# A streaming encoder layer with an expert mixer: state stores after the value weights' load, that load in halves, an earlier forget gate Exp, the mixer's loops written out, and the sample's queries in halves at later slots

## The chip, the cores and the metric

The kernel runs on one core of one Trainium2 chip. The metric is the device time of one execution in microseconds (us), lower is better. Three executions of the kernel before took 3363.31 to 3365.3 us, median 3364.35 us.

## The reference, cut to what matters

One layer over a prompt of 1024 tokens and a sample of 32 tokens, width 1024. A combined input projection feeds an RG-LRU group and an mLSTM group (4 heads of 128), an output projection closes the mixer of time, and a PEER block with 16384 experts closes the layer.

```python
def mlstm_chunk(carry, inp):              # per head, in chunks
    b = jnp.cumsum(lf, axis=-1)           # lf = log_sigmoid(forget gate)
    logD = jnp.where(causal, b[..., :, None] - b[..., None, :] + ig[..., None, :], -jnp.inf)
    m_t = jnp.maximum(inter, jnp.max(logD, axis=-1))
    ...
    C_new = w_c[..., None, None] * C + jnp.einsum('bhs,bhsd,bhse->bhde', w_k, k, v)

def peer(h, wq, k1, k2, u, v):            # 8 heads, 16 experts a head and token
    q = (xb @ wq).reshape(PEER_BLOCK, PEER_HEADS, D_QUERY)
    q = q * lax.rsqrt(jnp.mean(q * q, axis=-1, keepdims=True) + EPS)
    s1 = jnp.einsum('phd,kd->phk', q1, k1); s2 = jnp.einsum('phd,kd->phk', q2, k2)
    v1, i1 = lax.top_k(s1, 16); v2, i2 = lax.top_k(s2, 16)
    sv, si = lax.top_k((v1[..., :, None] + v2[..., None, :]).reshape(..., 256), 16)
    expert = e1 * N_KEYS + e2
    g = jax.nn.softmax(sv, axis=-1)
    act = jax.nn.gelu(jnp.einsum('phkd,pd->phk', jnp.take(u, expert, axis=0), xb))
    return jnp.einsum('phk,phkd->pd', g * act, jnp.take(v, expert, axis=0))

def trunk_layer(...):
    h = rmsnorm(x, norm1_w) * (1.0 + sc1) + sh1
    z = h @ w_in + b_in
    ya, h_last, conv_new = rglru(...); yb, C, n, m = mlstm(...)
    x = x + g1 * (jnp.concatenate([ya, yb], axis=-1) @ w_out)
    h2 = rmsnorm(x, norm2_w) * (1.0 + sc2) + sh2
    return x + g2 * peer(h2, ...), h_last, conv_new, C, n, m
```

## The kernel before, in words

The order of the work is written out by hand, one program for each engine, and semaphores tie the programs together. The 1056 tokens stand in 9 tiles (`NT`): 8 of 128 prompt tokens and one of 32 sample tokens.

**First part.** PE (TensorE) multiplies 16 blocks of 128 columns of the input projection (`lb`, line 686): the LRU's xa and ga, then q and k. The key blocks k0 to k3 come last; behind k1 stand the input and forget gates (line 697). ACT (ScalarE) evicts each block (lines 1031 and 1033). Then come the value and output-gate columns, `value_gate`, in 18 units: most are 8 products of 128x512 (line 743), the unit for the sample tile is 32 products of 128x256 (line 737) and needs both weight halves, `wo` and `wv`. `wo` is loaded early; `wv` takes the SBUF slots 4 to 7 of the block weights and is loaded by SP (line 424) once block k3 is done (`z_mm` at `VO`, 51). DVE (VectorE) adds the biases and evicts (lines 1483 and 1492); a PSUM bank must be evicted before PE's unit four later may start in it.

The forget gate's log-sigmoid needs |f| (DVE, line 1510), Exp of it (ACT, line 1087), then a log1p of 13 operations on 4 rows of 1056 (DVE, lines 1300 to 1308). In DVE's program this stands ahead of the first eviction, `evict_vo(0)`. In ACT's program the Exp stands behind all block evictions.

POOL (GpSimd) issues the small transfers. Ten of them (`store`, line 508) write the LRU states to HBM, column by column of SBUF, so that each element is a piece of 4 bytes of its own: two of 128x4 and eight of 128x3. They stand ahead of `top_dram` (line 516) and of its broadcast back, `top_b` (line 536). Later `store_state(1, 1)` writes the sample's mLSTM state, and DVE's `carry(1)` (line 1593) waits for 14 stores together (`SAMPLE_STORES`) before it overwrites that state. Then follow mLSTM, output projection and second norm over the 9 tiles, with PE's program the longest.

**Second part, the mixer.** A slot is one expert of each token of a tile: POOL gathers 128 rows of 8 KB (line 588, an indirect DMA of 1 MB) into one of 8 ring buffers, DVE takes the dot product with the token (`dot`, line 1809), ACT makes the weight and puts it on a diagonal (`weight`, lines 1232 to 1240), and PE multiplies the diagonal with the second half of the rows into PSUM (`mix`, line 915), which frees the buffer (`v_free`). There are 128 slots a prompt tile (8 heads h of 16 slots j) and 32 for the sample tile, 1056 in all. In between, two heads ahead, PE makes the next queries (`query`, line 884) and scores (lines 904, 906) and DVE sorts them (`route` steps). ACT's `query` (line 1199) copies the query out of PSUM; it stands behind `weight` of slot 0. At `h == S_AT` (5) of the head two ahead, that is while head 3 is mixed, `query` also multiplies the sample's 32 tokens with this tile's head of weights (line 891, 16 products of 128x32 in one piece), in eight tiles once.

`each_tile` sets the tiles in the programs of POOL, ACT and DVE: tile 0, then a hardware loop of three rounds of two tiles (1 to 6), then tiles 7 and 8. SP has a loop of its own around `finish`. PE's program is written out.

```python
            tile(0, 0, P, P)
            with eng.Fori(0, (NT - 3) // 2) as i:
                tile(i * 2 + 1, 1, P, P)
                tile(i * 2 + 2, 0, P, P)
            tile(NT - 2, 1, P, DEC)
            tile(NT - 1, 0, DEC, None)
```

## Time and profile before

| | |
|---|---|
| median of three executions | 3364.35 us |
| the profiled execution | 3363.62 us |
| its span, first to last instruction | 3361.8 us |
| PE busy, weight loads | 86%, 42% |
| DVE, ACT, POOL busy | 66%, 64%, 36% |
| moved by DMA | 1191.56 MB, of it 1118.53 MB by POOL's queue |
| instruction fetches in the span | 264 packets, 2.80 MB |

The span is cut into two: the first 610 us or so, in which PE is busy nearly all the time and DMA little, and the mixer behind it, in which the DMA engines are busy in nearly every slice and every other engine has gaps. A busy share over the whole span mixes both.

### The profile page before, as it was taken

What the parts mean: (1) busy time and instruction counts of PE and PEld (TensorE: products, weight loads), DVE (VectorE), ACT (ScalarE), POOL (GpSimd) and SP (SyncE); (2) the same over time, 40 slices, a digit from 0 to 9 for tenths busy, and PEclk for the clock granted to TensorE, in tenths of its full rate; (3) what the DMA queues carried; (4) which work ended last, traced back from release to release, by engine and by line L of the source; (5) the groups of instructions that cost most, each with busy time, mean ns of one, the idle gap of its engine ahead of it and who ended that gap; (6) DMA issues with size and microseconds to landing.
All of it is one profiled execution on the core that took longest, in us unless ns stands there. A gap on an engine that the chain in (4) does not pass through costs nothing. (4 is left out here: it accounts for less than half of the span.)

```text
span 3361.8 us, 42448 instructions
## 1 busy us (share of the span) xinstructions
PE 2888.0 (86%) x9454; PEld 1410.6 (42%) x9454; DVE 2231.8 (66%) x5472; ACT 2150.2 (64%) x7214; POOL 1206.9 (36%) x1134
## 2 busy tenths in 40 slices
PE   7998999788888888888888888888888888888886
PEld 5664455434434443343344334343443343434331
DVE  5685355667676667666666676666666766676665
ACT  3332133477776777677667776777777777777775
POOL 0001000244444444344435444444444444434443
PEclk9999999899999999999999999999999999999999
DMA  7233032799999999999999999999999999999998
GB/s 280 85 114 62 30 119 79 322 420 412 419 417 414 396 419 409 407 411 419 389 413 415 419 417 394 419 419 387 402 420 419 415 392 419 420 415 400 420 419 330
DMA packets 169996, 1191.56 MB, mean 354 GB/s; under 512 B 20027, under 2 KB 21467, under 8 KB 30211
## 3 DMA queue, kind: packets, MB, share of 16 engines
q0 software_dynamic: 155792, 1118.53, 81.0%
q1 hardware_dynamic: 13940, 70.23, 5.9%
q8 instruction: 78, 1.28, 0.2%
q14 instruction: 186, 1.52, 0.1%
HBM read 1179.42 MB, written 9.25 MB: 354 GB/s over the span
## 5 line engine op out<-in xcount | busy, mean ns | idle before, releaser
L915 PE MATMUL ps<-r_w,r_yT 128*128 128x512 f32 (+1 forms) x3168 | 1525.7, 616 | 329.7 <-ACT r_yT L1240 326.5
L1809 DVE SCALAR_TENSOR_TENSOR r_yT<-r_w,r_qk 128x1024 bf16<-128x1024 f32 x792 | 968.9, 1225 | 683.8 <-DMA r_w<-in_peer_uv,gidx 682.7
L588 POOL DMA_INDIRECT r_w<-in_peer_uv,gidx x792 | 872.9, 1102 | 1018.1 <-PE ps L915 895.4
L915 PEld LDWEIGHTS ps<-r_w,r_yT 128*128 128x128 f32 (+1 forms) x3168 | 551.8, 189 | 1216.0 <-issue 1214.9
L915 PE MATMUL ps<-r_yT 128*128 128x512 f32 (+1 forms) x1056 | 526.6, 633 | 87.3 <-ACT r_yT L1240 76.1
L588 POOL DMA_INDIRECT r_yT<-in_peer_uv,gidx x264 | 291.6, 1104 | 559.3 <-PE ps L915 490.9
L1232 ACT ACTIVATE mixc<-mixc 128x1 f32<-128x1 f32 x1056 | 207.2, 196 | 441.3 <-DVE r_yT L1809 437.6
L1240 ACT ACTIVATE r_yT<-ident,mixc 128x128 f32<-128x128 f32 x1024 | 411.2, 402 | 97.7 <-ACT mixc L1236 5.1
L1236 ACT ACTIVATE mixc<-mixc 128x1 f32<-128x1 f32 x1056 | 409.1, 387 | 35.0
L1235 ACT ACTIVATE mixc<-mixc 128x1 f32<-128x1 f32 x1056 | 408.3, 387 | 33.8
L1809 DVE SCALAR_TENSOR_TENSOR r_yT<-r_yT,r_qk 128x1024 bf16<-128x1024 f32 x264 | 322.9, 1225 | 119.2 <-DMA r_yT<-in_peer_uv,gidx 102.5
L915 PEld LDWEIGHTS ps<-r_yT 128*128 128x128 f32 (+1 forms) x1056 | 198.7, 202 | 377.2 <-issue 376.8
L1234 ACT ACTIVATE mixc<-gate,mixc 128x1 f32<-128x1 f32 x1056 | 295.8, 280 | 0.0
L686 PE MATMUL ps<-r_hT,r_w 128*128 128x384 f32 (+1 forms) x768 | 232.8, 465 | 2.1 <-DVE r_hT L1403 1.8
L1233 ACT ACTIVATE mixc<-mixc 128x1 f32<-128x1 f32 x1056 | 198.3, 188 | 0.0
L686 PEld LDWEIGHTS ps<-r_hT,r_w 128*128 128x128 f32 x768 | 146.6, 192 | 87.0 <-issue 6.2
L1199 ACT ACTIVATE r_yT<-ps 128x256 f32<-128x256 f32 x64 | 24.5, 383 | 174.6 <-PE ps L884 129.9
L884 PEld LDWEIGHTS ps<-r_wq,r_vo 128*128 128x128 f32 x1024 | 120.9, 194 | 14.9 <-issue 14.8
L884 PEld LDWEIGHTS ps<-r_wq,r_hT 128*128 128x128 f32 x1024 | 119.4, 192 | 15.3 <-issue 15.3
L884 PE MATMUL ps<-r_wq,r_vo 128*128 128x128 f32 x1024 | 121.2, 277 | 0.0
L884 PE MATMUL ps<-r_wq,r_hT 128*128 128x128 f32 x1024 | 119.5, 275 | 0.0
L743 PE MATMUL ps<-r_w,r_hT 128*128 128x512 f32 x256 | 111.2, 593 | 0.0
(287 smaller groups left out, 2321.3 us busy)
## 6 DMA issues: line engine op xcount, KB each, us to landing
r_w<-in_ada_w SPq DMA_DIRECT2D x18, 1024.0 KB, 5.2
r_w<-in_peer_uv,gidx POOLq DMA_INDIRECT x792, 13.8
r_w<-in_w_lin SPq DMA_DIRECT2D x16, 512.0 KB, 7.4
r_yT<-in_peer_uv,gidx POOLq DMA_INDIRECT x264, 11.8
r_vo<-in_x_prompt SPq DMA_DIRECT2D x8, 512.0 KB, 7.3
r_qk<-in_ada_w SPq DMA_DIRECT2D x2, 2048.0 KB, 16.8
r_w<-in_w_vo SPq DMA_DIRECT2D x2, 2048.0 KB, 13.1
r_w<-in_w_out SPq DMA_DIRECT2D x2, 2048.0 KB, 8.4
```

The source lines that it names most:

```text
L588: pool.indirect_dma_start(ring[place(h, j)], None, table, bass.IndirectOffsetOnAxis(gidx_t[:, h, j:j + 1], 0))\
L686: m = nc.tensor.matmul(ps[:, bank, 0:n], wblk[:, nblk % 8, k, :], hT[:, k, c0:c0 + n], start=k == 0, stop=k == KD - 1)
L743: m = nc.tensor.matmul(ps[0:r, bank, :], hT[:, k, t * P:t * P + r], w[:, k, :], start=k == 0, stop=k == KD - 1)
L884: mm = nc.tensor.matmul(ps[:, 4, c * P:(c + 1) * P], wqs[h][:, k, c * P:(c + 1) * P], h2T[:, p, k, :], start=k == 0, stop=k == KD - 1)
L915: mm = nc.tensor.matmul(ps[0:r, 2 * p + c, :], diag[:, j % 4, 0:r], row[:, D + c * 512:D + (c + 1) * 512], start=h == 0 and j == 0, stop=h ...
L1232: nc.scalar.activation(sq[:, i:i + 1], d, ACT.Square, scale=(TANH_K * GELU_C) ** 0.5)
L1233: nc.scalar.activation(kd[:, i:i + 1], d, ACT.Copy, scale=TANH_K)
L1234: wch.link(nc.scalar.activation(gd[:, i:i + 1], gate_t[:, h, j:j + 1], ACT.Copy, scale=d))
L1235: wch.link(nc.scalar.activation(th[:, i:i + 1], sq[:, i:i + 1], ACT.Tanh, scale=d, bias=kd[:, i:i + 1]))
L1236: wch.link(nc.scalar.activation(wc[:, i:i + 1], th[:, i:i + 1], ACT.Identity, scale=gd[:, i:i + 1], bias=gd[:, i:i + 1]))
L1240: nc.scalar.activation(diag[:, j % 4, 0:r], (ident if r == P else sel32)[:, 0:r], ACT.Copy, scale=wc[:, i:i + 1]).then_inc(dg_ready, 1)
L1809: V.scalar_tensor_tensor(udump[j % 2], ring[i][:, 0:D], 1.0, h2[:, t, :], ALU.mult, ALU.mult, accum_out=dots[:, i:i + 1]).then_inc(dot_don ...
```

## The change

- **Stores.** The ten LRU state stores stand in POOL's program behind the broadcast of `top_b`, and wait for both halves of `wv` first.
- **Value weights.** `wv` is loaded in two halves: slots 4 and 5 once block k1 is done (`z_mm` 42), slots 6 and 7 once k3 is done (51). PE's first use waits for both (32).
- **Forget gate.** ACT's Exp stands behind the eviction of k2, ahead of that of k3.
- **Mixer.** `each_tile` has no loop: the programs of POOL, ACT and DVE hold all nine tiles, and SP's `finish` loop is written out as well.
- **Sample queries.** `S_AT` is 4, now the head being mixed; the 16 products stand in two pieces of 8, behind `mix` of slots 6 and 10. ACT copies them behind `weight` of slot 13, and PE waits for that copy before the query of the next head.

```diff
-S_AT = 5
+S_AT = 4
...
+        def each_tile(tile):
+            for t in range(NT):
+                tile(t, t % 2, rows(t), rows(t + 1) if t + 1 < NT else None)
...
-            for n, dst in ((1, wo), (0, wv)):
-                if n:
-                    sp.wait_ge(half_done[0], 8)
-                    sp.wait_ge(half_done[1], 8)
-                else:
-                    sp.wait_ge(z_mm, VO)
-                sp.dma_start(dst, A["w_vo"][n].rearrange("p (k n) -> p k n", k=KD)).then_inc(vo_ld[n], 16)
+            sp.wait_ge(half_done[0], 8)
+            sp.wait_ge(half_done[1], 8)
+            sp.dma_start(wo, A["w_vo"][1].rearrange("p (k n) -> p k n", k=KD)).then_inc(vo_ld[1], 16)
+            w_v = A["w_vo"][0].rearrange("p (k n) -> p k n", k=KD)
+            for q, blocks in enumerate((42, VO)):
+                sp.wait_ge(z_mm, blocks)
+                sp.dma_start(wv[:, 4 * q:4 * q + 4], w_v[:, 4 * q:4 * q + 4]).then_inc(vo_ld[0], 16)
...
             finish(0, P, x1_t[0], y_t[0])
-            sp.wait_ge(y_st, 16)
-            with sp.Fori(1, NT - 2) as t:
+            for t in range(NT - 2):
                 finish(t, P, x1_t[t], y_t[t])
...
             pool.dma_start(top_b, top_dram[:, :].partition_broadcast(P)).then_inc(top_ld, 16)
+            pool.wait_ge(vo_ld[0], 32)
             pool.wait_ge(lru_y, 2 * FT)
             for s in range(2):
                 store(outs[2 + 5 * s][0, 0].rearrange("(f p) -> p f", p=P), hl[:, s, :])
                 for f in range(FT):
                     store(outs[3 + 5 * s][0, 0, :, f * P:(f + 1) * P].rearrange("r p -> p r"), cvn[:, s, f, :])
...
-                if h == S_AT:
-                    if t == 0:
-                        pe.wait_ge(s_ev, 1)
-                    for c in range(2):
-                        for k in range(KD):
-                            mm = nc.tensor.matmul(ps[:, 4, 2 * P + c * DEC:2 * P + (c + 1) * DEC],
-                                                  wqs[t][:, k, c * P:(c + 1) * P], h2Ts[:, k, :],
...
+            def query_for_sample(t, c):
+                if t == 0:
+                    pe.wait_ge(s_ev, 1)
+                for k in range(KD):
+                    mm = nc.tensor.matmul(ps[:, 4, 2 * P + c * DEC:2 * P + (c + 1) * DEC],
+                                          wqs[t][:, k, c * P:(c + 1) * P], h2Ts[:, k, :],
+                                          start=k == 0, stop=k == KD - 1)
+                if c == 1:
+                    mm.then_inc(s_tr, 1)
...
+                    if h == S_AT + 1 and t < NT - 1:
+                        pe.wait_ge(s_ev, t + 2)
...
+                        if h == S_AT and t < NT - 1 and j in (6, 10):
+                            query_for_sample(t, j // 10)
...
+                if b == "k2":
+                    act.wait_ge(f_abs, 1)
+                    nc.scalar.activation(nmr, wst, ACT.Exp, scale=-1.0).then_inc(f_exp, 1)
...
-            act.wait_ge(f_abs, 1)
-            nc.scalar.activation(nmr, wst, ACT.Exp, scale=-1.0).then_inc(f_exp, 1)
...
+                        if r == P and h == S_AT and j == 13:
+                            queried_for_sample(t)
```

The issues of POOL, behind the last block of the projection; `out<-prm` are state stores. Before:

```order
L503 DMA r_wq<-in_state_mlstm_n 128x4x1
L508 DMA out<-prm 128x4x1
L508 DMA out<-prm 128x3x1 x4
L508 DMA out<-prm 128x4x1
L508 DMA out<-prm 128x3x1 x4
L516 DMA top_dram<-r_yT 4x1056
L508 DMA out<-prm 4x1 x2
L536 DMA r_yT<-top_dram 128x4224
L542 AFFINE_SELECT r_hT<-r_hT 32x4x32
```

Now:

```order
L497 DMA r_wq<-in_state_mlstm_n 128x4x1
L505 DMA top_dram<-r_yT 4x1056
L502 DMA out<-prm 4x1 x2
L525 DMA r_yT<-top_dram 128x4224
L502 DMA out<-prm 128x4x1
L502 DMA out<-prm 128x3x1 x4
L502 DMA out<-prm 128x4x1
L502 DMA out<-prm 128x3x1 x4
L538 AFFINE_SELECT r_hT<-r_hT 32x4x32
```

The ten stores of columns moved from ahead of `top_dram` to behind the load of `top_b`; the causal cut of the decays stands right behind them.

ACT at the end of the projection; `r_qk<-ps,prm` evicts a key block, the row on `r_w` of 4x1056 is the forget gate's Exp. Before:

```order
L1031 ACTIVATE r_qk<-ps,prm 128x3x128 x2
L1031 ACTIVATE r_qk<-ps,prm 128x2x128
L1033 ACTIVATE r_qk<-ps,prm 128x32
L1087 ACT_TABLE_LOAD
L1087 ACTIVATE r_w<-r_w 4x1056
L1084 ACTIVATE r_vo<-r_vo 32x512
```

Now:

```order
L1083 ACT_TABLE_LOAD
L1083 ACTIVATE r_w<-r_w 4x1056
L1033 ACTIVATE r_qk<-ps,prm 128x3x128 x2
L1033 ACTIVATE r_qk<-ps,prm 128x2x128
L1035 ACTIVATE r_qk<-ps,prm 128x32
L1089 ACTIVATE r_vo<-r_vo 32x512
```

The Exp with its table load passed the three evictions of k3.

PE in tile 1 of the mixer, at the sample's query; rows on `r_w` or `r_yT` of 128x512 are `mix`, two of them a slot, 128x128 x16 is a query, 128x32 the sample's. Before:

```order
L915 MATMUL ps<-r_yT 128x512 x4
L915 MATMUL ps<-r_w,r_yT 128x512 x12
L884 MATMUL ps<-r_wq,r_hT 128x128 x16
L891 MATMUL ps<-r_hT,r_vo 128x32 x16
L915 MATMUL ps<-r_yT 128x512 x4
```

Now:

```order
L914 MATMUL ps<-r_w,r_yT 128x512 x8
L889 MATMUL ps<-r_hT,r_vo 128x32 x8
L914 MATMUL ps<-r_w,r_yT 128x512 x2
L914 MATMUL ps<-r_yT 128x512 x4
L914 MATMUL ps<-r_w,r_yT 128x512 x2
L889 MATMUL ps<-r_hT,r_vo 128x32 x8
L914 MATMUL ps<-r_w,r_yT 128x512 x10
L880 MATMUL ps<-r_wq,r_hT 128x128 x16
```

The sample's products left the place behind an ordinary query, and stand in two pieces four slots apart in the next head.

## Rows read from the trace of the kernel before

**Rows 1.** Windows in the mixer: length, busy by engine, granted clock, DMA share, GB/s

```profile
660.00:760.00 100.00, 86.11 (x264) 40.31 (x263) 68.64 (x180) 70.56 (x247) 43.23 (x40) 0.98 1.01 419
...
760.00:800.00 40.00, 36.03 (x128) 18.46 (x127) 29.70 (x79) 29.33 (x105) 16.56 (x16) 1.00 1.00 405
1080.00:1120.00 40.00, 36.35 (x134) 19.45 (x134) 27.06 (x69) 28.86 (x104) 17.93 (x16) 0.96 0.91 373
1410.00:1450.00 40.00, 36.01 (x134) 18.61 (x132) 26.57 (x68) 28.47 (x102) 17.07 (x16) 1.00 0.95 377
1740.00:1780.00 40.00, 35.24 (x133) 18.86 (x134) 27.59 (x72) 28.33 (x103) 16.42 (x15) 1.00 1.00 399
2070.00:2110.00 40.00, 37.24 (x135) 19.68 (x134) 26.56 (x71) 28.81 (x105) 17.06 (x16) 0.96 0.93 384
2405.00:2445.00 40.00, 38.29 (x134) 20.30 (x132) 25.24 (x68) 27.80 (x101) 17.38 (x15) 0.91 0.96 384
2735.00:2775.00 40.00, 37.42 (x135) 19.50 (x133) 26.02 (x69) 28.45 (x102) 19.17 (x16) 0.96 0.93 378
3060.00:3100.00 40.00, 36.08 (x136) 19.43 (x135) 27.57 (x72) 28.76 (x105) 17.06 (x15) 1.00 0.96 381
```

**Rows 2.** The same view at three of the tiles' boundaries

```profile
1600.00:1660.00 60.00, 47.68 (x131) 21.18 (x130) 43.97 (x113) 42.46 (x145) 24.87 (x22) 0.94 0.94 376
2260.00:2320.00 60.00, 50.83 (x133) 22.96 (x134) 43.65 (x111) 42.92 (x147) 25.05 (x22) 0.91 0.94 374
1300.00:1360.00 60.00, 49.13 (x140) 21.57 (x139) 42.21 (x112) 45.38 (x148) 24.45 (x23) 0.97 1.00 404
```

**Rows 3.** Timeline, tile 1 at the sample's query: start, length, engine, line [idle before <-releaser]

```profile
1089.60 3.66 PE L891 MATMUL ps<-r_hT,r_vo 128*128 128x32 f32 x32
...
1093.29 0.38 ACT L1199 ACTIVATE r_yT<-ps 128x256 f32<-128x256 f32 x1 [5.50 <-PE ps L891]
...
1097.27 1.57 POOL L588 DMA_INDIRECT r_yT<-in_peer_uv,gidx  x1 [9.27 <-PE ps L915]
```

**Rows 4.** The same view, POOL at an ordinary head of tile 2

```profile
1463.30 0.94 POOL L588 DMA_INDIRECT r_yT<-in_peer_uv,gidx  x1 [4.29 <-PE ps L915]
```

**Rows 5.** The same view, DVE where the loop goes back to tile 3

```profile
1625.27 1.23 DVE L1809 SCALAR_TENSOR_TENSOR r_yT<-r_yT,r_qk 128x1024 bf16<-128x1024 f32 x1 [6.56 <-issue]
```

**Rows 6.** Landing times of line 424's two loads, SP's `wo` and `wv`

```profile
DMA to landing us min/median/max: 7.3/13.1/18.9
```

**Rows 7.** Timeline of PE, a value unit, the sample unit, and a shape like it

```profile
305.13 7.03 PE L743 MATMUL ps<-r_w,r_hT 128*128 128x512 f32 x16
...
324.40 5.86 PE L737 MATMUL ps<-r_w,r_hT 128*32 128x256 f32 x64 [12.24 <-DMA r_w<-in_w_vo]
...
458.68 1.91 PE L822 MATMUL ps<-r_w,r_hT 128*32 128x256 f32 x32
```

**Rows 8.** Window over that sample unit, columns as in Rows 1

```profile
324.40:330.20 5.80, 5.80 (x65) 3.06 (x65) 5.63 (x6) 0.00 (x0) 0.00 (x0) 0.61 0.01 3
```

**Rows 9.** Timeline of ACT and DVE around the forget gate

```profile
291.50 0.28 ACT L1033 ACTIVATE r_qk<-ps,prm 128x32 f32<-128x32 f32 x1
...
306.00 1.28 ACT L1087 ACT_TABLE_LOAD   x1
...
308.41 0.70 DVE L1300 TENSOR_SCALAR r_w<-r_w 4x1056 f32<-4x1056 f32 x1 [21.67 <-ACT r_w L1087]
...
331.47 0.69 DVE L1492 TENSOR_TENSOR r_vo<-ps,r_wr 128x512 f32<-128x512 f32 x1
```

**Rows 10.** Line 508, landing times of its last two LRU stores

```profile
DMA to landing us min/median/max: 24.1/25.2/26.4
```

**Rows 11.** Timeline, line 508's LRU stores, `top_b`, and DVE's `carry(1)`

```profile
285.34 7.44 POOL L508 DMA_DIRECT2D out<-prm  x10
...
388.38 0.56 POOL L536 DMA_DIRECT2D r_yT<-top_dram  x1 [28.40 <-PE ps L713]
...
431.20 1.50 DVE L1593 SCALAR_TENSOR_TENSOR r_wq<-r_wq,prm,ps 128x129 f32<-128x129 f32 x4
```

More of the change, by code:

```diff
@@ L536, in _ @@
             pool.dma_start(top_b, top_dram[:, :].partition_broadcast(P)).then_inc(top_ld, 16)
+            pool.wait_ge(vo_ld[0], 32)
+            pool.wait_ge(lru_y, 2 * FT)
+            for s in range(2):
+                store(outs[2 + 5 * s][0, 0].rearrange("(f p) -> p f", p=P), hl[:, s, :])
+                for f in range(FT):
+                    store(outs[3 + 5 * s][0, 0, :, f * P:(f + 1) * P].rearrange("r p -> p r"), cvn[:, s, f, :])
             def cut_future(i):
@@ L590, in tile @@
                             .then_inc(e_ld[place(h, j)], 16)
-            each_tile(pool, tile)
+            each_tile(tile)
             pool.wait_ge(out_st, n_out[0])
@@ L949, in tile @@
                             scores(ta, ha)
+                        if h == S_AT and t < NT - 1 and j in (6, 10):
+                            query_for_sample(t, j // 10)
                         if rn == P and h == 5 and j in (4, 10):
                             turn(t + 1, j // 10, rn)
-            for t in range(NT):
-                tile(t, t % 2, rows(t), rows(t + 1) if t + 1 < NT else None)
+            each_tile(tile)
         @block.scalar
@@ L1199, in query, with queried_for_sample @@
                 nc.scalar.activation(qts[:, :, :], q, ACT.Copy)
-                if h == S_AT:
-                    for c in range(2):
-                        nc.scalar.activation(qs[c].rearrange("p (h t) -> p h t", h=HEADS)[:, t, :],
+                nc.scalar.activation(qsq[:, :, :], q, ACT.Square).then_inc(q_sb, 1)
+            def queried_for_sample(t):
+                act.wait_ge(s_tr, t + 2)
+                for c in range(2):
+                    m = nc.scalar.activation(qs[c].rearrange("p (h t) -> p h t", h=HEADS)[:, t, :],
                                              ps[:, 4, 256 + c * DEC:256 + (c + 1) * DEC], ACT.Copy)
-                nc.scalar.activation(qsq[:, :, :], q, ACT.Square).then_inc(q_sb, 1)
+                m.then_inc(s_ev, 1)
             def query_sample(h):
@@ L1274, in tile @@
                             norm(number(ta, ha))
-                        if h == 0 and j == 8 and (not isinstance(t, int) or t >= 1):
-                            final_root(t + (-1))
+                        if h == 0 and j == 8 and t >= 1:
+                            final_root(t - 1)
                         if rn == P and h == 5 and j in (7, 13):
                             turned(t + 1, j // 13, 1 - p, rn)
-            each_tile(act, tile)
+                        if r == P and h == S_AT and j == 13:
+                            queried_for_sample(t)
+            each_tile(tile)
             final_root(NT - 1)
@@ L1874, in tile @@
                     n = number(t, h)
-                    fin = h == 0 and (not isinstance(t, int) or t >= 1)
+                    fin = h == 0 and t >= 1
                     dot(t, h, 0)
@@ L1913, in tile @@
                     if fin:
-                        final_scale(t + (-1), P)
+                        final_scale(t - 1, P)
                     if ra:
@@ L1927, in tile @@
                         experts(ha)
-            each_tile(dve, tile)
+            each_tile(tile)
             final_sum(NT - 1, 0, DEC)
```

34 lines of the change are left out of this document (10 added, 24 removed).

## The prediction

> **What bounds the kernel now.** I read the windows first, then the timeline at the places where a window falls off. In the mixer an undisturbed window moves 419 GB/s with the DMA engines full (share 1.01) [rows 1]. A slot is a gather of 128 rows of 8 KB, 1.05 MB, so it takes 1.05 MB / 419 GB/s = 2.50 us, and 1056 of them take 2640 us: four fifths of the profiled execution. In the same window PE is busy 86 of 100 us, ACT 71 and DVE 69, so none of them sets the pace. The time of the mixer changes only where the DMA engines run dry. That happens at two kinds of place.
>
> Once in each of eight tiles a window of 40 us falls to 373 to 405 GB/s [rows 1]. The timeline shows why: the sample's products keep PE for 3.66 us behind an ordinary query, ACT waits 5.50 us for them before it may go on to the next weights, no ring buffer comes free, and POOL sits 9.27 us without issuing a gather [rows 3]. At an ordinary head, with its own query of 16 products but without the sample's, POOL sits 4.29 us [rows 4], and the windows show no loss. So the gathers already queued cover a gap of about 4 us and not one of 9.
>
> At the starts of tiles 3 and 5, where the loop goes back, windows of 60 us fall to 376 and 374; at the start of tile 2, inside the loop's body, a like window has 404 [rows 2]. DVE stands 6.56 us on "issue", that is on nothing but its own program, ahead of the first dot product behind the jump [rows 5].
>
> Ahead of the mixer PE is the long program, and it has one large hole: 12.24 us for `wv` [rows 7]. The two loads of line 424 are of equal size and took 7.3 and 18.9 us [rows 6]; the slow one waits for k3, behind which PE goes on at 305.13 [rows 7], while the ten LRU stores of 4-byte pieces, issued from 285.34 on [rows 11], are still landing: the last two take 24.1 and 26.4 us [rows 10], to about 318 us.
>
> **The change part by part.** The sum is made against the profiled execution, 3363.62 us, which is 0.7 us under the median of 3364.35; I take them as one.
>
> *Stores and `wv`: 12.2 us.* Without the stores `wv`'s first half lands long before it is wanted. The second half is issued at about 305.2 us as before; PE wants it at 324.40 - 12.24 = 312.16 us. Half the bytes can hardly take longer than the 7.3 us of the whole undisturbed load, and 305.2 + 7.3 = 312.5, so at most 0.3 us of the wait is left and I take none. The Trainium skill, page DMA: Bandwidth & Descriptors, section Anatomy of one DMA, gives (for DMAs of POOL) each DMA a fixed cost of about 2.0 us beside its bytes. That speaks against loading in halves; by its fit the second half takes about 4.4 us, an estimate from the page, and is hidden all the same.
>
> *Clock: 2.0 us.* Behind the hole the sample unit ran at a mean granted clock of 0.61 [rows 8], partly at the lower level of 1.2 GHz, after PE had stood idle; its 64 instructions took 5.86 us, while 32 of the like shape later took 1.91 us [rows 7], so 3.8 us for 64 [rows 7]. With no hole there is nothing to fall from.
>
> *Forget gate: nothing by itself, but it guards these 14 us.* DVE's log1p starts at 308.41, when the Exp is done, and DVE's first eviction is at 331.47 [rows 9]. If the hole went alone, PE would do the sample unit to 316.0, one value unit of 7.03 us [rows 7] to 323.0, and then stand for the bank of unit 0, evicted at about 332.2: 9.2 us of 14.2 would come back as that wait. Now the Exp follows k2's eviction: 291.50 + 0.28, then load and Exp for 308.41 - 306.00 = 2.4 us [rows 9], so 294.2, before k3's first group is there. DVE starts 14.2 us earlier and evicts at 317.3. PE needs that bank at 323.0 and has 5 us in hand. ACT's wait for |f| costs nothing, since DVE was waiting for the Exp from 308.41 - 21.67 = 286.7 on.
>
> *Stores in their new place: +1.0 us.* Everything behind the hole moves 14.2 us up: `top_b` is issued at 374.2, the stores follow for 7.44 us of POOL [rows 11], covered by `top_b`'s landing, for which the decays and the causal cut wait anyway. The old batch took from 285.34 to 318.4 to land, 33 us, `wv` beside it in part; behind `top_b` the new one ends at 408 to 416. `store_state(1, 1)` queues behind it, and `carry(1)`, due at 431.20 - 14.2 = 417.0 [rows 11], waits for all 14. That wait is 0 to about 5 us on DVE; behind DVE stand evictions that PE wants some microseconds later. Bounds 0 and 5, taken 1, being nearer to no wait.
>
> *Sample queries: 23.5 us.* The eight windows lack 14, 46, 42, 20, 35, 35, 41 and 38 GB/s of 419, together 271; times 40 us / 419 is 25.9 us of empty DMA [rows 1]. A piece is half of 3.66 us [rows 3], 1.83 us; PE's spare time is 14 us in 100 us, or 0.35 us a slot, so four slots take back 1.4 us between the pieces. The gap that reaches POOL is then near the ordinary 4.29 us and not 9.27, and ACT's copies, behind slot 13, wait for nothing. PE's new wait ahead of the next query is for a copy issued two slots before. Bounds: 25.9 if nothing is left, 13 if the two pieces leave half. I take 0.3 us left a tile, 23.5.
>
> *Loops: 10.4 us.* The two windows lack 43 and 45 GB/s over 60 us: 6.2 + 6.4 = 12.6 us. What an ordinary boundary costs is between 0 and the 15 GB/s of tile 2's, 2.1 us [rows 2]; I leave 1.1 us at each. Bounds 8.3 and 12.6. The instructions executed are the same, and the page's totals show 264 fetch packets for all 42448 of them, loop rounds included, so there is no more to fetch. SP's loop waits for nothing that another engine feels.
>
> Sum: 12.2 + 2.0 - 1.0 + 23.5 + 10.4 = 47.1 us. 3363.6 - 47.1 = 3316.5; forecast **3316.5 us**.
>
> **The rivals.**
> 1. *The pieces stall as well* (10%). Head 4 also has ACT's table loads for the norm at slot 6, and PE's backlog of two pieces may add to them. For it: a gap of 9.27 us runs the queue dry and 4.29 does not, and the limit between is not shown. Against: each piece is shorter than an ordinary query. Half the gain gone: 3316.5 + 12 = 3328.5.
> 2. *The jump is not what costs* (7%). The Trainium skill, page Advanced Engine Details and Errata, section Control Flow Timing, puts a compare-and-branch at about 108 ns; by that the edge would be cheap. As a mechanism of this kernel: DVE's stall is a fetch of instructions that straight code would meet as well. Against: DVE's stall stands right at the jump [rows 5], and the other edge's window reads like this one's, while tile 2's start, with no jump, reads 404 [rows 2]. Then 10.4 us stay: 3326.9. The row contradicts the page's figure if that is taken as the whole cost of an edge.
> 3. *The early gain is handed back* (10%). The store batch delays `carry(1)` by its full 5 us, or PE meets a bank not evicted. Half of 13.2: 3323.1.
> 4. *Slower than before* (2%). Straight programs for DVE, ACT and POOL may stall at each refill of their instructions while the DMA queues are full. The place is tiles 1 to 6; the price of a stall is DVE's 6.56 us [rows 5]. It decides from eight stalls on, 52 us against the other 47: at two a tile, 12 x 6.56 = 79, less the 10.4 that the loop no longer saves counted in, 3316.5 + 79 = 3395. Against it: tile 0 and tiles 7 and 8 are straight code already, and the window in tile 0 has 419 GB/s [rows 1].
> 5. *More than forecast* (8%): no residue at all, 3316.5 - 2.4 - 2.2 - 1.0 = 3310.9.
>
> **How the numbers follow.** The forecast itself has 63%; its terms alone span 3311 to 3323. For 8 in 10 I take in rivals 1, 2 and 3 and the lower side: **3307 to 3330 us**. What can be told from no change here is 0.2%, 6.7 us. Only rival 4, or several losses together, reach that: faster 0.95, same 0.02, slower 0.03.
>
> **What would show it.** PE has no wait for `wv` and the window behind 312 us a granted clock of 1.0; the first gathers come 13 us earlier; DVE's log1p starts at about 294 us. The eight windows and both edges read 410 GB/s or more; POOL's longest waits for PE in them are near 4.3 us. DVE has no "issue" idle over 2 us in the mixer. I am wrong if the windows fill but the mixer ends no earlier, if `carry(1)` waits over 5 us, or if new "issue" stalls appear on DVE or POOL.

## The result and the profile after

| | before | changed |
|---|---|---|
| median | 3363.83 us (4 runs, 3358.73 to 3365.30) | 3335.80 us (4 runs, 3334.78 to 3337.14) |
| ratio | | 0.992, 95% interval 0.9902 to 0.9937 |
| span of the profiled execution | 3361.8 us | 3334.8 us |

The change wins 28 us where the forecast was 47.1 and the range ended at 3330. The direction is right, the size is not.

The page of the changed kernel, its first lines and the two queues of instruction fetches:

```profile
span 3334.8 us, 38192 instructions
...
PE 2874.9 (86%) x9454; PEld 1405.6 (42%) x9454; DVE 2227.1 (67%) x5472; ACT 2155.5 (65%) x7214; POOL 1210.1 (36%) x1134
...
q8 instruction: 78, 1.28, 0.2%
q14 instruction: 140, 1.15, 0.1%
```

Queue q8 fetches PE's instructions, q14 those of DVE, ACT and POOL: in the experiments below q8 grows with PE's instructions alone and q14 with each of the others'. The page of before counts 42448 instructions, and 186 packets in queue q14. The loops had cost 4256 executed instructions and 46 fetches.

**Ahead of the mixer** everything reads as forecast. PE in the changed kernel, the timeline over the place of the old hole [rows 7]:

```profile
304.01 7.03 PE L739 MATMUL ps<-r_w,r_hT 128*128 128x512 f32 x16
310.97 3.66 PE L733 MATMUL ps<-r_w,r_hT 128*32 128x256 f32 x64
314.56 55.20 PE L739 MATMUL ps<-r_w,r_hT 128*128 128x512 f32 x128
```

DVE there, at the forget gate [rows 9] and at `carry(1)` [rows 11], and POOL's first gather:

```profile
293.09 0.70 DVE L1309 TENSOR_SCALAR r_w<-r_w 4x1056 f32<-4x1056 f32 x1 [7.87 <-ACT r_w L1083]
...
417.26 1.49 DVE L1602 SCALAR_TENSOR_TENSOR r_wq<-r_wq,prm,ps 128x129 f32<-128x129 f32 x4
```

```profile
597.56 1.93 POOL L584 DMA_INDIRECT r_yT<-in_peer_uv,gidx  x1 [17.35 <-PE ps L829]
```

PE doesn't wait for `wv`, the sample unit takes 3.66 us and not 5.86, DVE goes on at 293.09 (forecast 294.2), `carry(1)` waits for nothing, and the first gather is issued 12.6 us earlier than before's 610.19.

**In the mixer** the windows of the forecast, moved up by 13 us. Here the steady one and the eight at the sample's queries [rows 1], then the three boundaries [rows 2]:

```profile
660.00:760.00 100.00, 86.44 (x279) 41.57 (x280) 70.04 (x179) 72.63 (x258) 41.60 (x39) 1.00 1.01 420
747.00:787.00 40.00, 33.20 (x99) 14.98 (x98) 29.98 (x79) 29.22 (x103) 17.03 (x16) 1.00 1.01 420
1067.00:1107.00 40.00, 33.47 (x103) 15.31 (x102) 26.82 (x69) 29.37 (x102) 16.30 (x16) 1.00 1.01 415
1397.00:1437.00 40.00, 33.52 (x103) 15.31 (x101) 26.75 (x71) 29.36 (x102) 17.04 (x16) 1.00 1.01 418
1727.00:1767.00 40.00, 33.86 (x104) 15.49 (x102) 26.82 (x71) 29.22 (x103) 18.41 (x17) 1.00 1.01 417
2057.00:2097.00 40.00, 33.45 (x99) 14.92 (x98) 26.82 (x73) 28.89 (x102) 18.03 (x16) 1.00 1.01 418
2392.00:2432.00 40.00, 33.51 (x103) 15.55 (x103) 27.68 (x72) 28.85 (x100) 18.22 (x16) 1.00 1.01 419
2722.00:2762.00 40.00, 34.86 (x104) 16.03 (x103) 27.68 (x72) 28.92 (x100) 16.87 (x17) 0.96 1.01 413
3047.00:3087.00 40.00, 35.25 (x104) 16.62 (x104) 27.77 (x73) 29.59 (x105) 16.74 (x16) 0.96 1.01 412
1587.00:1647.00 60.00, 51.35 (x149) 23.40 (x148) 45.27 (x114) 43.30 (x148) 27.43 (x25) 0.97 1.00 408
2247.00:2307.00 60.00, 51.37 (x164) 24.55 (x162) 44.34 (x107) 43.00 (x146) 25.84 (x23) 0.97 0.99 401
1287.00:1347.00 60.00, 49.99 (x141) 22.39 (x139) 43.23 (x116) 46.43 (x152) 27.85 (x24) 0.97 1.00 408
```

The eight windows are full: they lack 21 GB/s together where they lacked 271. POOL's longest wait for PE in the window of tile 2, in the timeline:

```profile
1406.73 0.94 POOL L584 DMA_INDIRECT r_yT<-in_peer_uv,gidx  x1 [4.20 <-PE ps L914]
```

That is an ordinary head's gap [rows 4], where it was 9.27 us at the sample's query of tile 1 [rows 3].

Yet from the first to the last complete landing of a gather the mixer takes 2717.7 us where it took 2732.0, 14 us less and not 34. That is near the sign that the prediction named for being wrong, windows that fill while the mixer ends no earlier. The loss has moved into the stretches between. Windows of before between two sample events, where nothing was wrong:

```profile
790.00:1080.00 290.00, 246.05 (x743) 114.37 (x741) 200.21 (x516) 211.73 (x733) 123.40 (x114) 0.98 1.01 417
...
1450.00:1600.00 150.00, 126.28 (x401) 59.99 (x402) 102.05 (x262) 109.79 (x383) 63.30 (x60) 1.00 1.01 419
...
2110.00:2260.00 150.00, 127.85 (x403) 60.42 (x401) 101.78 (x263) 109.71 (x382) 66.59 (x60) 0.99 1.01 419
```

The same places in the changed kernel:

```profile
777.00:1067.00 290.00, 250.54 (x773) 119.76 (x773) 200.35 (x517) 212.25 (x737) 125.23 (x114) 0.98 1.01 415
...
1437.00:1587.00 150.00, 132.37 (x434) 65.70 (x435) 101.82 (x265) 111.08 (x386) 64.39 (x59) 0.98 1.01 412
...
2097.00:2247.00 150.00, 130.71 (x434) 64.89 (x433) 101.01 (x265) 111.95 (x390) 63.46 (x58) 0.99 1.01 412
```

The DMA share is 1.01 in all of them. A mean over 16 engines doesn't tell that one of them is late. The landing records do: a gather lands in 16 parts, one for each DMA engine. The table shows, read from these records, how far the first and the last part of one gather lie apart, and the time from one slot's last part to the next's:

```
                     first to last part   last part to last part
                     (median, us)         (mean of slots 150 to 1040, us)
before               3.61                 2.578
changed              5.46                 2.562
undisturbed slot                          2.49
```

The same records show what a stall does to the last part. Three of the eight sample queries of the kernel before, each at its longest gap, and the sum of the five intervals around each of the eight queries over 2.494 us an interval:

```
                         first part to first part   last part to last part
before, tile 1                    7.81 us                  2.68 us
before, tile 2                    5.57                     2.49
before, tile 4                    6.57                     2.70
before, eight queries            32.1 over                 6.6 over
changed, eight queries            1.1 over                 2.9 over
```

The first parts lose 31 us more in the kernel before than in the changed one, the last parts 3.6. The last part of each gather comes late, and at these gaps it goes on coming every 2.5 to 2.7 us while the first parts stand.

### The profile page after: what moved, and what is told of

It reads as the page before. It is cut to its first block and busy times, and to the rows that moved or that the text cites. A ratio compares the mean times of both kernels' runs of the same rounds, so it can differ in the third digit from the quotient of the medians.

```text
span 3334.8 us, 38192 instructions
## 1 busy us (share of the span) xinstructions
PE 2874.9 (86%) x9454; PEld 1405.6 (42%) x9454; DVE 2227.1 (67%) x5472; ACT 2155.5 (65%) x7214; POOL 1210.1 (36%) x1134
## 5 line engine op out<-in xcount | busy, mean ns | idle before, releaser
L914 PE MATMUL ps<-r_yT 128*128 128x512 f32 (+1 forms) x1056 | 510.2, 615 | 79.0 <-ACT r_yT L1247 77.3
## 6 DMA issues: line engine op xcount, KB each, us to landing
r_yT<-in_peer_uv,gidx POOLq DMA_INDIRECT x264, 12.2
```

What stands on the lines that cost most here:

```text
L914: mm = nc.tensor.matmul(ps[0:r, 2 * p + c, :], diag[:, j % 4, 0:r], row[:, D + c * 512:D + (c + 1) * 512], start=h == 0 and j == 0, stop=h ...
```

## The experiments

The first four kernels set the prediction's sum (theory A) against the first thing that these records suggest: a late DMA engine catches up while the others stand still in a stall, so a stall costs less than its empty time (theory B). Runs of one kernel lie 2 to 10 us apart, its medians in the four groups of runs 3362.2 to 3365.5 for the kernel before, and a ratio's interval is about 0.0015, or 5 us, each way. The twelve kernels that have the changed kernel's program ahead of the mixer, itself among them, still show their first landing at 600.9 to 605.5 us, so some 4 us of a difference between two of them can come from ahead of the mixer. Where less than that matters the text also gives the mixer's length, from the first to the last complete landing of a gather, which lies between 2715.8 and 2718.8 us in ten unrolled kernels (the changed one, a2, a3, b1, b3, b4, c1, c3, c4, d4).

**The early edits alone (a1).** The kernel before with the stores behind `wv`, `wv` in halves and the Exp behind k2.

> The kernel before with only the three edits ahead of the mixer (stores behind wv, wv in halves, forget gate's Exp behind k2); mixer, loops and sample queries as before. Both theories expect the first gathers about 13 us earlier. Theory A (prediction: nothing behind the start changes): 3363.8 - 13.2 = 3350.6. Theory B (slowest DMA engine sets the mixer's pace) expects the same, 3351. Rival (the early gain is handed back in the mixer): 3357 to 3364.

Measured 3352.39 us, ratio 0.9967 (0.9955 to 0.998). 10.8 us under before, and both theories hold. The first gather's landing came at 603.9 us against 616.8, 12.9 us earlier, and the mixer took 2734.5 us against 2732.0. Those 2.5 us are not clear of the noise.

**The mixer's edits alone (a2).**

> The changed kernel with its three early edits undone: only the unrolled mixer and the sample queries in halves. Theory A (the sum of the prediction): 3363.8 - 33.9 = 3330. Theory B (each stall let the slowest DMA engine catch up, so only the part of it beyond that is won): 3335.8 + 13 = about 3349, 15 us under the kernel before.

Measured 3346.44 us, ratio 0.9951 (0.9938 to 0.9965). The mixer's edits win 17 us and not 34. Theory A is out by 16 us here and by 2 us in a1, of the 19 us that the forecast missed by.

**The sample's query whole again (a3).**

```diff
-S_AT = 4
+S_AT = 5
...
+                if h == S_AT:
+                    for c in range(2):
+                        for k in range(KD):
+                            mm = nc.tensor.matmul(ps[:, 4, 2 * P + c * DEC:...
...
-                        if h == S_AT and t < NT - 1 and j in (6, 10):
-                            query_for_sample(t, j // 10)
```

> The changed kernel with the sample's query whole again behind the ordinary query of head 5; the loops stay unrolled. Theory A: the eight windows lose 271 GB/s times 40 us again, so 3335.8 + 23.5 = 3359. Theory B: the spread of the landings is reset by each of the eight stalls, about half comes back: 3335.8 + 8 to 12 = 3346, and each later stretch up to the next stall is faster than in the changed kernel.

Measured 3336.24 us, ratio 0.9919 (0.9905 to 0.9932): the changed kernel's time within 0.5 us, and its mixer within 1.1 (2718.8 us). The halves, the largest term of the forecast, are worth nothing that can be told from noise. That is less than theory B gave them too. Its windows, two of the eight sample events and then the stretches behind them:

```profile
1397.00:1437.00 40.00, 36.50 (x136) 19.60 (x136) 27.07 (x72) 28.55 (x104) 16.21 (x16) 1.00 0.97 386
...
2057.00:2097.00 40.00, 35.72 (x134) 18.86 (x133) 26.50 (x71) 29.14 (x103) 17.18 (x16) 1.00 0.97 387
...
1437.00:1587.00 150.00, 127.60 (x402) 60.70 (x401) 101.82 (x264) 110.86 (x384) 64.61 (x58) 0.99 1.01 419
...
2097.00:2247.00 150.00, 127.57 (x405) 60.85 (x404) 101.18 (x263) 110.80 (x384) 65.19 (x59) 1.00 1.01 419
```

The stall is back (386 GB/s for the changed kernel's 418), and the stretch behind it has its 419 again, where the changed kernel has 412. 32 GB/s over 40 us are 3.1 us of empty DMA, 7 GB/s over 150 us are 2.5. What the stall takes, the stretch gives back.

**The loops back (a4).**

```diff
-            for t in range(NT):
-                tile(t, t % 2, rows(t), rows(t + 1) if t + 1 < NT else None)
+            tile(0, 0, P, P)
+            with eng.Fori(0, (NT - 3) // 2) as i:
+                tile(i * 2 + 1, 1, P, P)
+                tile(i * 2 + 2, 0, P, P)
```

> The changed kernel with the hardware loops back on every engine; sample queries stay in halves. Theory A: 3335.8 + 10.4 = 3346. Theory B: the spread is reset at two edges, 3335.8 + 4 to 7 = 3341. Rival C (the straight program itself costs something in tiles 1 to 6 by its instruction fetches): equal to the changed kernel or faster, 3330 to 3336.

Measured 3349.93 us, ratio 0.9962 (0.9948 to 0.9975). Unrolling is worth 14.1 us, nearly all that the mixer won; with loops the halves are worth 2.5 us (3352.39 - 3349.93), which isn't clear of the noise. Theory A's 3346 is nearer than theory B's 3341, and rival C is refuted: straight code doesn't cost. What unrolling removes beside the jumps is 4256 instructions, 46 fetches in q14. So a theory F: the slowest DMA engine is the one that also carries instruction fetches. Theory J, its rival, has the jumps alone cost. The next four kernels change instructions that nobody waits for.

**Fewer idle instructions (b1).**

```diff
-                        pool.sem_inc(pool_turn, 1)
...
-                pe.sem_inc(pe_turn, 1)
...
-                dve.sem_inc(dve_turn, 1)
+                pass
```

> The changed kernel without the semaphore increments that nobody waits for (one per slot on POOL and PE, one per hold on DVE): some 3000 instructions less to fetch, the work is the same. Theory F (the mixer's end is set by the DMA engines that also carry the instruction fetches; 44 fetch packets fewer in the mixer were what unrolling won, 13 us): about 0.3 us less per packet of 8 KB and 1.0 us per packet of PE's 16 KB, in all 3335.8 - 5 to 12 = 3327. Theory J (the loops' edges cost by their jumps alone, 6.5 us each; fetches cost nothing): 3335.8, within 2 us.

Measured 3332.86 us, ratio 0.9909 (0.9894 to 0.9925). 3 us faster, between the two; the mixer itself is only 1.3 us shorter (2716.4), and its first landing 2.6 us earlier, so this run alone decides nothing.

**More idle instructions, on DVE (b2), on POOL (b3), on PE (b4).**

```diff
                                        accum_out=dots[:, i:i + 1]).then_inc(dot_done, 1)
+                for _ in range(4):
+                    dve.sem_inc(dve_turn, 1)
```

> The changed kernel with four idle semaphore increments more behind every dot product of DVE, some 4200 instructions or 33 fetches of 8 KB more, on an engine that waits for data in every slot. Theory F: 33 x 0.31 = 10 us slower, 3346. Theory J: no change, 3336.

POOL's stand ahead of the gather in the same form, PE's beside its own in `mix` and `scores`.

> The changed kernel with four idle semaphore increments more ahead of every gather on POOL: also some 33 fetches of 8 KB more. Theory F: as for DVE, 10 us slower, 3346. Theory J: no change, 3336. If only this one of the two is slower, it is POOL's own time to issue and not the fetches.

> The changed kernel with three idle semaphore increments more at each of PE's two places that have one, some 3200 or more instructions, or 13 to 17 fetches of 16 KB more. Theory F: 13 to 17 times about 1.0 us, 3349 to 3353. Theory J: no change, 3336.

Measured 3375.10 us on DVE (ratio 1.0035, 1.0021 to 1.0048), 3335.36 on POOL (0.9918, 0.9904 to 0.9931) and 3337.24 on PE (0.9924, 0.9910 to 0.9937). 33 more fetches cost 39 us if they are DVE's and nothing that can be told from noise if they are POOL's; 14 more of PE's 16 KB cost nothing either. So neither F nor J stands: the cost is not of fetches in general, it came with DVE's. The view of DMA between 700 and 3100 us shows that the count alone says nothing. DVE's kernel:

```profile
DMA packets 135571, 980.28 MB, mean 408 GB/s; under 512 B 15056, under 2 KB 15056, under 8 KB 16880
...
q14 instruction: 143, 1.17, 0.1%
```

POOL's, with more packets:

```profile
DMA packets 137430, 993.85 MB, mean 414 GB/s; under 512 B 15261, under 2 KB 15261, under 8 KB 17085
...
q14 instruction: 145, 1.19, 0.1%
```

The landing records show how it comes about. In the changed kernel 803 of 890 intervals from last part to last part are 2.45 to 2.53 us, and outside the slots where a tile's x1 and y move, 43 are over 2.9 us, 21 slots apart in the median. DVE executes 6.04 instructions a slot, 128 in 21.2 slots. In those 43 intervals the last part alone is late: it comes 3.46 us after the slot before's in the mean, the last but one of the 16 parts 2.53. So one DMA engine falls behind, and the others don't. Two such places in DVE's timeline of the changed kernel, the dot product in front and the late one each:

```profile
2060.89 1.22 DVE L1818 SCALAR_TENSOR_TENSOR r_yT<-r_w,r_qk 128x1024 bf16<-128x1024 f32 x1 [1.26 <-DMA r_w<-in_peer_uv,gidx]
...
2064.42 1.23 DVE L1818 SCALAR_TENSOR_TENSOR r_yT<-r_w,r_qk 128x1024 bf16<-128x1024 f32 x1 [1.62 <-DMA r_w<-in_peer_uv,gidx]
...
2116.73 1.23 DVE L1818 SCALAR_TENSOR_TENSOR r_yT<-r_yT,r_qk 128x1024 bf16<-128x1024 f32 x1 [0.86 <-DMA r_yT<-in_peer_uv,gidx]
...
2120.20 1.23 DVE L1818 SCALAR_TENSOR_TENSOR r_yT<-r_w,r_qk 128x1024 bf16<-128x1024 f32 x1 [1.38 <-DMA r_w<-in_peer_uv,gidx]
```

3.53 and 3.47 us from start to start, for the 2.49 us of the slots around them; 22 slots lie between. The table from the landing records and the executed instructions:

```
kernel         DVE executes   intervals over 2.9 us   sum over 2.494 us
changed         7206          43                      41.4 us
fewer idle      6678          38                      37.0
more on DVE    11430          70                      67.4
more on POOL    7206          42                      40.7
more on PE      7206          42                      40.7
```

0.96 us each, and between them nothing has changed: the median interval is 2.49 us in all five. If the idle instructions cost by lengthening the way from a landing to the freed buffer, every interval would be longer. With POOL's and PE's more instructions 42 of the 43 long intervals stand at the very slots of the changed kernel. 33 fetches by 0.96 us are 32 of the 39 us; the other 7 I can't account for. This is theory D (each fetch of DVE makes the last part 0.96 us late), and it foretells what taking instructions from DVE gives.

**Dot products in place (c1).** The product's dump goes over the half of the gathered row that nobody reads afterwards, so the wait on its own `dot_done` falls away in every slot; the idle increments stay out.

```diff
-                if s >= 2:
-                    dve.wait_ge(dot_done, s - 1)
-                V.scalar_tensor_tensor(udump[j % 2], ring[i][:, 0:D], 1.0, h2[:, t, :], ...
+                V.scalar_tensor_tensor(ring[i][:, 0:D], ring[i][:, 0:D], 1.0, h2[:, t, :], ...
```

> The changed kernel with the dot product's dump written over the half of the gathered row that nobody reads afterwards, so that DVE's wait on its own dot_done falls away in every slot, and without the idle semaphore increments. DVE executes about 1570 instructions less than in the changed kernel, 12.3 blocks of 128. Theory D (each block of 128 instructions of DVE costs the last landing 0.96 us: 43 jumps in 890 slots with the changed kernel, 70 with four idle increments more per dot product; blocks of POOL and PE cost nothing): 3335.8 - 12 = 3324. Rival (DVE's added increments were slower by DVE's own time in the chain from a landing to the freed buffer, not by fetches): within 3 us of the kernel without idle increments, 3330 to 3333.

Measured 3330.70 us, ratio 0.9904 (0.9888 to 0.9919); the mixer 2717.0 us, no shorter. A miss for D, and by the time alone the rival's number. The long intervals are still there, but 17 slots apart, and 16.8 slots are what ACT needs for 128 of its 7.6 instructions a slot.

**More idle instructions on ACT (c2).**

```diff
                                      scale=wc[:, i:i + 1]).then_inc(dg_ready, 1)
+                for _ in range(4):
+                    act.sem_inc(act_turn, 1)
```

> The changed kernel with four idle semaphore increments on ACT behind every slot's last copy: 4224 instructions, 33 blocks of 128 more. Theory D with DVE alone on the slowest DMA engine: no change, 3336, since ACT's 7.5 instructions a slot against DVE's 6 already show no jumps of their own. Rival (any engine that stands in the chain from landing to freed buffer costs by its time): 3350 to 3375, as with DVE. Rival (ACT's blocks load the same DMA engine): about 3368.

Measured 3356.28 us, ratio 0.998 (0.9971 to 0.9989): 20 us slower, which theory D excluded and its first rival, the time of an engine on the way from landing to freed buffer, allowed. Against that rival the median interval is again 2.49 us, and the long intervals stand 11 slots apart, as ACT now executes 128 instructions in 11.0 slots. So ACT's fetches do cost, only not in the changed kernel. A fetch can be told by its engine, since it comes when that engine's count of executed instructions stands near 64 in a block of 128. By how much the interval behind a fetch is longer, on average, over fetches of one engine without the other's near:

```
kernel          behind a DVE fetch     behind an ACT fetch
changed         0.86 us (34 of them)   0.07 us (42)
fewer idle      0.90 (31)              0.04 (39)
more on DVE     0.96 (57)              0.04 (40)
in place        0.03 (8)               0.62 (49)
more on ACT     0.03 (35)              0.62 (65)
```

Where one of the two costs, the other costs nothing. That suggests two DMA engines, one late by DVE's fetches and one by ACT's, of which the later sets the pace (theory D2). With ACT in front an interval over 2.9 us is 0.70 us too long (50 of them, 35.0 us, in place; about 80 of them, 56 to 60 us, with more on ACT, where two slots in five lack landing records and the count is rough). By that ACT's 63 fetches in the mixer (8021 instructions / 128) come to 44 us and DVE's 50 (6369 / 128) to 48 us: in the changed kernel DVE's is in front and ACT's close behind, and relieving DVE alone can win no more than 4 us. In place, the mixer is 0.7 us shorter than the changed kernel's and 0.6 longer than that with fewer idle instructions.

**The fewest instructions (d1).** ACT is relieved too: eight diag buffers for four, and one wait in four slots.

```diff
-                act.wait_ge(v_free, s + 5)
-                nc.scalar.activation(diag[:, j % 4, 0:r], ...
+                if j % 4 == 0:
+                    act.wait_ge(v_free, s + 4)
+                nc.scalar.activation(diag[:, j % 8, 0:r], ...
```

> The kernel without idle increments and with dot products in place, and now also eight diag buffers for four, so that ACT waits for one only in every fourth slot: ACT executes 792 instructions less (6.2 blocks of 128). Theory D2 (two DMA engines carry DVE's and ACT's instruction blocks, each block costs that engine 0.9 us, the slower of the two sets the pace; with DVE relieved it is ACT's): 3330.7 - 5 = 3326. Rival (another limit stands at 2717 us of mixer whatever the instructions): 3330 to 3332.

Measured 3326.20 us, ratio 0.9891 (0.9876 to 0.9906), the mixer 2709.2 us: D2's number. It does the same work 9.6 us faster than the changed kernel, 8.5 us of it in the mixer. The edit also doubles the diag buffers, which could win time by itself. The long intervals speak for the fetches: they now stand 19 slots apart, ACT executes 128 instructions in 18.7 slots, and their sum is 28.9 us, 6.1 less than in place, of the 7.8 us by which the mixer is shorter. In every one of these kernels the spacing follows the instructions of one engine, and of that engine alone:

```
kernel         long intervals apart   128 instructions of DVE   of ACT
               (median, slots)        take (slots)              (slots)
changed        21                     21.2                      16.8
fewer idle     23                     23.1                      16.8
more on DVE    13                     12.8                      16.8
in place       17                     27.8                      16.8
more on ACT    11                     21.2                      11.0
fewest         19                     27.8                      18.7
```

Of the changed kernel's two engines it is DVE that sets the spacing, though ACT fetches more often. That fits a cost of 0.96 us for the one and 0.70 for the other.

The DMA view of the kernel with the fewest, 700 to 3100 us (the changed kernel has 414 GB/s and 116 packets of q14 there):

```profile
DMA packets 137779, 996.31 MB, mean 415 GB/s; under 512 B 15306, under 2 KB 15306, under 8 KB 17130
...
q14 instruction: 92, 0.75, 0.1%
```

**The loop on DVE alone (d2), on ACT alone (d3).** The diff is the one of the loops back, for one engine.

> The changed kernel with the hardware loop on DVE alone. It adds 970 instructions (7.6 blocks) on DVE and its two jumps. Theory D2: 7 us by the blocks and up to 6 by the jumps, 3343 to 3349. Prediction's theory (an edge costs 5.2 us where DVE stands on its jump): 3346. Rival (ACT's instructions cause all of the loops' cost): 3336.

> The changed kernel with the hardware loop on ACT alone: 2419 instructions more on ACT (19 blocks), and no jump on DVE. Theory D2: 33 blocks more of ACT cost 20 us, so 19 cost 8 to 14: 3344 to 3350. Prediction's theory (the cost of the loops is DVE's 6.56 us on its jump): 3336 to 3338.

Measured 3352.02 us with DVE's loop (ratio 0.9965, 0.9951 to 0.9978) and 3348.11 with ACT's (0.9955, 0.994 to 0.997): 16 and 12 us slower than the changed kernel, and 14 with all loops. They don't add up, and under D2 they needn't: only the later DMA engine counts. Both have a jump of their own; where DVE's loop goes back to tile 3:

```profile
1612.47 1.23 DVE L1828 SCALAR_TENSOR_TENSOR r_yT<-r_yT,r_qk 128x1024 bf16<-128x1024 f32 x1 [6.49 <-issue]
```

and where ACT's does, in the kernel with ACT's loop:

```profile
1606.81 0.20 ACT L1249 ACTIVATE mixc<-mixc 128x1 f32<-128x1 f32 x1 [5.09 <-issue]
```

With DVE's loop the tiles that begin with a jump are 4.3 and 5.3 us longer than in the changed kernel, the other four of the loop 1.2 to 1.5 us. The added instructions are in all six tiles: at 1.3 us a tile they make 7.7 us, where 970 / 128 = 7.6 fetches by 0.96 make 7.3. That leaves 7.0 us for the two jumps, for which DVE stands 6.49 us each.

**One edit of the early part at a time (c3, c4, d4).**

```diff
-                if b == "k2":
-                    act.wait_ge(f_abs, 1)
-                    nc.scalar.activation(nmr, wst, ACT.Exp, scale=-1.0).then_inc(f_exp, 1)
...
+            act.wait_ge(f_abs, 1)
+            nc.scalar.activation(nmr, wst, ACT.Exp, scale=-1.0).then_inc(f_exp, 1)
             for i in range(NT - 2):
                 open_gate(i)
```

> The changed kernel with the forget gate's Exp back behind k3. Prediction's theory: PE waits for the bank of unit 0, 9.2 us of the 14.2 come back: 3335.8 + 9 = 3345. Rival (the Exp's move does nothing): 3336.

The ten stores move ahead of `top_dram`:

```diff
+            pool.wait_ge(lru_y, 2 * FT)
+            for s in range(2):
+                store(outs[2 + 5 * s][0, 0]...
             pool.wait_ge(top_done, 1)
```

> The changed kernel with the ten LRU stores back at their old place; wv stays in halves. Prediction's theory: the tiny stores are what slowed wv; its second half is slowed by about as much as the whole was, 3335.8 + 8 to 13 = 3344 to 3349. Rival (halving alone hides it): 3336 to 3338.

```diff
-            for q, blocks in enumerate((42, VO)):
-                sp.wait_ge(z_mm, blocks)
-                sp.dma_start(wv[:, 4 * q:4 * q + 4], w_v[:, 4 * q:4 * q + 4]).then_inc(vo_ld[0], 16)
+            sp.wait_ge(z_mm, VO)
+            sp.dma_start(wv, w_v).then_inc(vo_ld[0], 16)
```

> The changed kernel with wv in one load again, asked for behind k3 as before, the stores still behind it. By the prediction's row of 7.3 us for an undisturbed load, from 305.2 to 312.5 where PE wants it at about 311: 0.3 to 1.5 us of wait, so 3336 to 3338. Rival (the halves carry part of the gain): 3341 or more.

Measured 3345.71 us with the late Exp (ratio 0.9951, 0.9935 to 0.9966), 3345.67 with the stores in front (0.9953, 0.9936 to 0.9970), 3337.00 with one load (0.9919, 0.9904 to 0.9934). The first two agree with the prediction, and the third shows that the halves of `wv` win next to nothing. PE's timeline says why, for the late Exp:

```profile
331.93 18.36 PE L739 MATMUL ps<-r_w,r_hT 128*128 128x512 f32 x38 [9.40 <-DVE r_vo L1500]
```

for the stores in front:

```profile
318.89 5.29 PE L732 MATMUL ps<-r_w,r_hT 128*32 128x256 f32 x64 [7.67 <-DMA r_w<-in_w_vo]
```

and for one load:

```profile
312.74 3.66 PE L732 MATMUL ps<-r_w,r_hT 128*32 128x256 f32 x64 [0.74 <-DMA r_w<-in_w_vo]
```

9.40 us of wait for the bank where 9.2 were worked out. With the stores in front the clock costs 1.6 us on top of the 7.67: the 64 instructions behind the wait take 5.29 us, at a granted clock of 0.68, and not 3.66.

## Why the prediction was right and wrong

*Stores and `wv`*, *Clock*, *Stores in their new place* (12.2 + 2.0 - 1.0 = 13.2): right. The first gathers come 12.6 us earlier, and the edits alone win 10.8 us (a1), or 10.6 seen from the kernel without them (a2); what is missing to 13.2 is within the noise. The second half of `wv` landed 5.1 us after its issue, where the estimate was 4.4. `carry(1)` waits 0 us where 1.0 was taken. The clock gave 2.2 us (5.86 to 3.66) where 2.0 was taken. The undisturbed load of 2 MB takes 7.4 us by itself, so loading in one leaves PE a wait of 0.74 us and costs 1.2 us by the medians (d4), less than the noise; the hole was the stores' doing, and with them in front it is 7.67 us even with halves (c4).

*Forget gate*: right in place and size, 9.40 us for 9.2 (c3).

*Sample queries: 23.5 us*: wrong, and the failed step of the whole. Measured 0.4 us with the loops unrolled (a3), 2.5 with them (a4), neither clear of noise. The events were as described: POOL's gap falls from 9.27 to 4.2 us, and the eight windows fill. The conversion was wrong: "times 40 us / 419 is 25.9 us of empty DMA" is a mean over 16 engines taken for the time of the mixer. The gathers advance with the last of the 16, and in those stalls that one worked on and caught up: of 31 us that the first landings lost at the eight queries the last ones lost 3.6. The lower bound of 13 came from "the two pieces leave half"; nothing in it allowed for full windows that win nothing, so the true value lay outside. Under it lies the first step, *What bounds the kernel*: "a slot ... takes 1.05 MB / 419 GB/s = 2.50 us, and 1056 of them take 2640 us". That is what the fast DMA engines could do. A sum made afterwards for the slowest one is 1056 x 2.494 = 2634, plus 50 fetches of DVE x 0.96 = 48, plus 8 x 2.7 = 22 for the tiles' x1 and y (20 intervals, 18.8 us, in seven tiles), plus 14 that tile 0 is longer than the others: 2718, and 2717.7 was measured. The prediction put the fetches, the x1 and y transfers and tile 0's extra at nothing.

*Loops: 10.4 us*: the size came near, 14.1 measured (a4), for half of the reason, so in part by luck. The two edges come to 7.0 us with DVE's loop alone (d2), the added instructions to 7.7. But "the instructions executed are the same ... so there is no more to fetch" is false. The two pages say 42448 and 38192; the loops' arithmetic is 970 instructions on DVE and 2419 on ACT, and those are the instructions whose fetches cost. Added to the changed kernel's mixer, 7.0 and 7.7 give 2732.4 us for a kernel with loops and with stalls that cost nothing, and the kernel before took 2732.0.

The sum that was measured: 10.7 for the early part, 14.1 for the loops, 0.4 to 2.5 for the sample queries in halves, 25 to 27 of the 28.

The rivals: that the pieces stall as well (1) is refuted by the windows, and that half of the early gain is handed back (3) by a1, whose edits alone keep 10.8 of the 13.2 us. More than forecast (5) did not come. That the jump is not what costs (2) is refuted by the 6.49 us on the jump, which appear with DVE's loop and go with it. The Trainium skill, page Advanced Engine Details and Errata, section Control Flow Timing, has 108 ns for a compare-and-branch; the trace disagrees if that is read as the cost of a loop's edge. That straight code stalls (4) had nothing to it: DVE's issue waits ahead of its dot products in the mixer come to 0.5 us, and the changed kernel, all of it straight code, is the faster. What the straight code does cost is in the landings and not on an engine.

That the last part comes late once for every 128 instructions of DVE or ACT is shown by runs in either direction (b1, b2, c1, c2, d1). That the fetch packet itself does it is the reading that fits: the fetches come at that rate and just ahead of the late parts. Why a packet of 8 KB, itself 0.3 us long in the records, makes its DMA engine 0.96 us late stays open. That the DMA engines in question are two is inferred from the landing records, which don't name an engine. The Trainium skill, page DMA: Bandwidth & Descriptors, section Latency and other measured facts, says that two of the 16 DMA engines are usually slower when POOL issues, and guesses at their descriptor traffic. Here the last part of a gather comes every 2.492 us in the median, as the parts before it do: outside of fetches and the tiles' own transfers no engine falls behind. Whether the DMA engines that carry these fetches are the page's two can't be told from these records.

## What to carry to other kernels

When gathers or loads run on all DMA engines without a pause, read the spread of their landings before pricing a stall: empty time on a mean over 16 engines was worth almost nothing here as long as the last engine had work. To price a stall, ask how late the last engine is when it begins; put the stall back in a kernel that is otherwise the new one, as a3 does. And in such a kernel an instruction is not free even where its engine is idle: here 128 idle semaphore increments on DVE cost about 1 us. So it is worth trying to merge waits and to unroll loops that execute much register arithmetic, on the engine whose fetches are in front first and then on the next.

## What the runs showed of the hardware

- Fetches: DVE, ACT and POOL together fetch one packet of 8 KB for 128 instructions executed ((7206 + 8446 + 2210) / 128 = 139.5, and the page of the profile has 140), PE one of 16 KB for 256 (20205 / 256 = 78.9, and 78).
- Instructions for 33 more fetches on DVE cost 39 us (b2), on ACT 20 us (c2), on POOL nothing (b3), and for 14 more on PE nothing (b4); each late landing is one of the 16 parts of a gather.
- A stall of 7.81 us between first landings left 2.68 us between last landings (before, tile 1).
- Where a loop goes back, DVE stands 6.5 us and ACT 5.1 us on issue; DVE's longest ahead of a dot product in the changed kernel's mixer is 0.3 us.
- Ten stores of 4-byte pieces ahead of a load make it late: the second half of `wv`, 1 MB, landed 14.4 us after its issue behind them (c4), 5.1 us without them, and all 2 MB in 7.4 us (d4).
